# Reversing the column order in which TensorE streams the activations, and in which it writes PSUM

## The reference, cut to what matters

```python
def swiglu_ffn(h, w_gate_up, w_down):
    gate, up = jnp.split(h @ w_gate_up, 2, axis=-1)
    return (jax.nn.silu(gate) * up) @ w_down
...
u = h @ w_in                              # s5_mixer
val, gate = jnp.split(z @ w_glu, 2, axis=-1)
ckv = h @ w_kv_a; c_q = rms_norm(h @ w_q_a, q_a_norm)
q = c_q @ w_q_b; kv = c_kv @ w_kv_b
x = x + o @ mla_w_o[j]                    # and w_in_2, w_out_2 in the second block
```

## Time and profile before

| | |
|---|---|
| median of 3 runs | 1853.35 us (1852.85 to 1853.47) |
| profiled execution: span from the first to the last instruction | 1850.4 us |
| what the runs' median has beside that span | 2.95 us |
| TensorE matmul busy | 1793.4 us (97%), 8806 records |
| TensorE weight loads busy | 1379.8 us (75%) |
| VectorE, ScalarE, GpSimd busy | 1078.9 us (58%), 838.5 us (45%), 209.3 us (11%) |
| mean granted TensorE clock | 0.990 of full speed |

### The profile page before, as it was taken

The page is one execution under the profiler, slowest core; times in us unless marked ns, Lnnn a source line. Parts: engine busy times, 40 slices in busy tenths (PEclk is TensorE's granted clock), DMA queues, the critical chain, the costliest instruction groups (busy, mean ns, idle before and its releaser), DMA issues.

```text
span 1850.4 us, 24262 instructions
## 1 busy us (share of the span) xinstructions
PE 1793.4 (97%) x8806; PEld 1379.8 (75%) x8806; DVE 1078.9 (58%) x1752; ACT 838.5 (45%) x1404; POOL 209.3 (11%) x293
## 2 busy tenths in 40 slices
PE   9889999999999999999999999999999999999997
PEld 6777878888887766677888888868766777866675
DVE  8883454444434767755444434466576676577666
ACT  5423344443223667644444322233467633256763
POOL 7980000000000000000000000023000202300010
PEclk9989999999999999999999999999999999999999
DMA  6322223232333111122222233323211122311111
GB/s 212 89 74 80 91 91 102 91 102 88 94 100 105 49 32 30 50 69 92 101 93 99 93 92 95 107 75 109 69 57 51 53 80 87 108 58 58 46 58 57
DMA packets 58765, 152.14 MB, mean 82 GB/s; under 512 B 17152, under 2 KB 22048, under 8 KB 58672
## 3 DMA queue, kind: packets, MB, share of 16 engines
q1 hardware_dynamic: 55120, 148.21, 24.7%
q0 software_dynamic: 3552, 2.70, 0.5%
HBM read 143.73 MB, written 4.19 MB: 80 GB/s over the span
## 4 chain that ended last, share of the span: by engine, by line
PE 85%; DVE 6%; ACT 4%; POOL 3%; issue 2%; DMA 0%; SPq 0%; DVEq 0%; ACTq 0%; POOLq 0%
PE bank L2060 18%; PE bank L2062 18%; PE bank L2061 18%; PE bank L2561 3%; PE bank L2563 3%; PE bank L2562 3%; PE bank L2514 2%; PE bank L2543 2%; PE bank L2544 2%; PE bank L2545 2%; PE bank L2287 1%; DVE wl L1268 1%; PE bank L2315 1%; PE bank L2576 1%; PE bank L2301 1%
## 5 line engine op out<-in xcount | busy, mean ns | idle before, releaser
L1268 DVE TENSOR_TENSOR wl<-raw,wh 128x1024 fp32r<-128x1024 f32 (+3 forms) x280 | 325.0, 1161 | 481.1 <-ACT wh L686 477.9
L686 ACT ACTIVATE wh<-raw 128x1024 fp32r<-128x1024 f32 (+3 forms) x280 | 279.3, 998 | 568.4 <-PE bank L2062 498.3
L2060 PE MATMUL bank<-xH,wh 128*128 128x512 f32 x872 | 342.3, 393 | 0.6 <-DVE wl L1268 0.6
L2061 PE MATMUL bank<-xL,wh 128*128 128x512 f32 x872 | 339.6, 389 | 0.0
L2062 PE MATMUL bank<-xH,wl 128*128 128x512 f32 x872 | 339.6, 389 | 0.0
L2060 PEld LDWEIGHTS bank<-xH,wh 128*128 128x128 f32 x872 | 163.9, 188 | 36.6 <-issue 2.9
L2061 PEld LDWEIGHTS bank<-xL,wh 128*128 128x128 f32 x872 | 163.9, 188 | 34.6 <-issue 1.0
L2062 PEld LDWEIGHTS bank<-xH,wl 128*128 128x128 f32 x872 | 163.8, 188 | 34.2
L2060 PE MATMUL bank<-hidH,wh 128*128 128x512 f32 x352 | 137.4, 390 | 0.0
L2062 PE MATMUL bank<-hidH,wl 128*128 128x512 f32 x352 | 137.0, 389 | 0.0
L2061 PE MATMUL bank<-hidL,wh 128*128 128x512 f32 x352 | 137.0, 389 | 0.0
(11 more groups left out here) (455 smaller groups left out, 3355.6 us busy)
## 6 DMA issues: line engine op xcount, KB each, us to landing
raw<-w_gu_dram SPq DMA_DIRECT2D x88, 512.0 KB, 3.2
raw<-w_p_dram SPq DMA_DIRECT2D x64, 512.0 KB, 3.3
raw<-w_dn_dram SPq DMA_DIRECT2D x32, 448.0 KB, 3.3
raw<-w_glu_dram SPq DMA_DIRECT2D x16, 512.0 KB, 3.4
raw<-w_dn_dram SPq DMA_DIRECT2D x16, 512.0 KB, 3.6
raw<-w_out_dram SPq DMA_DIRECT2D x16, 512.0 KB, 3.2
raw<-w_in_dram SPq DMA_DIRECT2D x8, 512.0 KB, 7.7
raw<-w_o_dram SPq DMA_DIRECT2D x8, 512.0 KB, 3.3
```

Of the source, the lines that this page charges most:

```text
L686: nc.scalar.activation(wh[:, (st.base + u) % 2, 0:kts * P], raw[:, (st.base + u) % 4, 0:kts * P], ACT.Copy).then_inc(w_high, 1)
L1268: nc.vector.tensor_tensor(wl[:, s, 0:kts * P], raw[:, (st.base + u) % 4, 0:kts * P], wh[:, s, 0:kts * P].bitcast(F32), ALU.subtract).then_ ...
L2060: nc.tensor.matmul(bank, wh[:, s, w], hi[:, k, :], start=first and kt == 0, stop=False)
L2061: nc.tensor.matmul(bank, wh[:, s, w], lo[:, k, :], start=False, stop=False)
```

## The change

In the straight branch of `product` the streamed tile is read from column 511 down to column 0, and the bank is written from column 511 down to column 0. Column t of the tile still lands in column t of the bank. The weights, the order of the matmuls, their number, the waits and the signals are as before. All other matmuls keep their direction.

```diff
@@ product, straight branch
-                    nc.tensor.matmul(bank, wh[:, s, w], hi[:, k, :], start=first and kt == 0, stop=False)
-                    nc.tensor.matmul(bank, wh[:, s, w], lo[:, k, :], start=False, stop=False)
-                    ins = nc.tensor.matmul(bank, wl[:, s, w], hi[:, k, :], start=False, stop=last and kt == kts - 1)
+                    nc.tensor.matmul(bank[:, ::-1], wh[:, s, w], hi[:, k, ::-1], start=first and kt == 0, stop=False)
+                    nc.tensor.matmul(bank[:, ::-1], wh[:, s, w], lo[:, k, ::-1], start=False, stop=False)
+                    ins = nc.tensor.matmul(bank[:, ::-1], wl[:, s, w], hi[:, k, ::-1], start=False, stop=last and kt == kts - 1)
```

## The result

| | before | changed |
|---|---|---|
| median | 1853.2 us (1852.85 to 1853.47) | 1876.8 us (1875.55 to 1879.86) |
| ratio | | 1.0130, 95% interval 1.0118 to 1.0141 |
| span of the profiled execution | 1850.4 us | 1874.2 us |

The change makes the kernel 1.3% slower. The profiled execution of the changed kernel took 1875.96 us in all, 1.8 us more than its span. The prediction had put 2.95 us there, the difference between a median and the span of one execution; the 1.2 us between the two figures decide nothing.

A forecast was written before the change was run, and what follows sets the result against it. TensorE's pace was taken to bound the kernel. The one term, 4704 matmuls times a distance change of 0, added nothing to the 1850.4 us span; 2.95 us between median and span gave 1853.4 us, range 1835 to 1920 us.

The forecast's parts named there:

- What bounds the kernel: Whole kernel: TensorE's own pace sets the time, 97% busy; 1066 us, 58% of the span, hangs on the edited lines.
- the single term: Edited lines 2060 to 2062: 4704 matmuls times d, the change in distance between starts; 1 ns is 4.70 us.
- I take d = 0: Edited matmuls: distance between starts stays 226.6 ns, nothing changes beyond 0.2%; 1853.4 us, chance 0.51 including a normalised-away reversal.
- the repeated column: Warm-up matmuls, line 2200, stream one column 512 times at 0.433 us a pass, taken as showing an odd step costs nothing.
- Rival B: Edited matmuls: mirrored stream meets the weight load at a dearer position; 26.5 us, 1880 us, up to 1916; chance 0.23.
- coarse position does not matter: Feed-forward: weight slices at 0, 512, 1024 and 1536 B all run at 226.6 ns beside xH; argued against a dearer position.
- Rival C: Edited matmuls get faster: 744 on out-of-line tiles give -4.5 us, 1849 us; at most -56 us, 1797 us; chance 0.09.
- Rival D: SBUF fetch or PSUM write doesn't pair falling columns: full effect 950 us, 2804 us; partial 1920 to 2804; chance 0.17.

The follow-up runs named there:

- blocks_of_64: Against the kernel before, read and write of the 4704 matmuls go through 64-column (256 B) blocks in falling order, columns rising inside: 1853.0 us, ratio 0.9998.
- the second probe: Separate kernel, no reference result: rows of 48 float32 matmuls varying column order, position and weight columns; 226.7 ns between starts rising, 233.3 falling.
- the probe: Separate kernel, no reference result: rows of 48 matmuls, reads or writes reordered, float32 or bfloat16; float32 226.7 ns rising, 233.5 read falling, 226.9 write falling.

## Why the prediction was wrong in its forecast and right in its range

**What bounds the kernel, and the single term.** Right. Nothing but TensorE's pace changed, no cover existed, and the sum "4704 matmuls x d" is the loss: the changed lines took 27.2 us more, 5.8 ns each on average.

**"I take d = 0."** This step failed. Its reasons were that a falling stream touches the same aligned pairs and groups of columns, makes the same number of fetches, and that the repeated column shows no price. The first is shown to be free by itself: swapped pairs and falling order within 16 B cost nothing. What I left out is the order of the 16-byte pieces within 256 B, which blocks_of_64 and the groups of the second probe show to be the whole price; in the feed-forward d measured +6.7 ns. The second, the number of fetches, no run shows. The third reason rested on rows at the two-cycle pace, which have 2 ns beyond their columns' time where the edited lines have 13, and on a stream that never leaves its 16-byte piece; I should have given it no weight. It stood at 0.51 and should have been below B.

**Rival B.** It happened, at the price that I worked out from w_o: 26.5 us, 1880 us, against 27.2 us on the changed lines and 1876.8 us. I had it at 0.23, held down by "coarse position does not matter". That was read from slices at 0, 512, 1024 and 1536 B, all multiples of 256 B, and the second probe shows that positions repeat after 256 B (226.7 ns with the weights at 0 B and at 256 B), so those rows could not speak on it. Its mechanism was half right: a rising stream does depend on its position against the weights. But the falling stream does not get to 233.3 ns by starting at byte 2044, as a rising one does by lying 96 B off. It is there at nearly every position of stream and weights. So the price of B came true in part by luck: the row that I took it from was the rising pace at 96 B, 233.3 ns, and the other positions off the line would have given 228.8 to 234.5. That falling streams have one pace wherever they lie is also why w_o and w_glu hardly moved, which the sum for B had right by leaving out their 744 matmuls. The range held because it had been drawn to take in B.

**Rival C.** That no direction goes below 226.6 ns held in all positions and orders of 512 distinct float32 columns tried. Its smaller half, 4.5 us for the tiles that are out of line, was real, but came by moving the tiles (3 us), and not by the change.

**Rival D and the write.** Excluded at its full size on both sides: no order of 512 columns in these runs came near the two-cycle pace of 429 ns, two columns swapped within their pair are read at 226.7 ns and written at 227.7, and a falling write has 226.9. What is left of it on the read is the 6.7 ns of this change, below D's range. "PSUM — Partial Sum Buffer" of the Trainium skill, Specifications, was weighed against the change. For a step of 2 the probe agrees with it: 256 bfloat16 columns take 215.0 ns in place of 109.2. A step of -1 is not a non-contiguous write in that sense: 226.9 ns against 226.7. "SBUF — State Buffer" of the Trainium skill, Door 1, asks for two hits on a 16-byte line. The float32 read with a step of 2 has two hits and takes 229.7 ns for 256 columns where contiguous ones take 120.2, so the rule doesn't hold for that form; and the falling stream, which hits each line four times, pays all the same.

**Left open.** Shown is that the pace depends on order and position within 256 B, that for a rising stream the position of the weights counts, and that a bfloat16 stream with bfloat16 weights doesn't pay in any of the four directions tried. Not shown is what meets with what. A wait at some shared part of SBUF between the stream and the weight load would fit the relative position, but not that one weight column costs the falling stream as much as 128. One rival stands untested: no run has the weights in falling order beside a falling stream, so it may be the order of the two against each other that costs, and not the stream's own.

## What to carry to other kernels

Where matmuls of 4-byte streams of some 350 columns or more set the time, place the streamed tiles and the weights at the same position within 256 B and stream in rising order: 96 B of difference cost this kernel 33 us, and putting four tiles in line gave 3 us. A reversed PSUM write, a reversal of blocks of 256 B, swapped neighbours and a full reversal in bfloat16 were free here, so a reversal that is needed can be put there. And when a trace shows two paces for one instruction, the cheaper one is a favourable case that an edit can lose: such a row belongs to the forecast and not only to the range.

## What the runs showed of the hardware that was not expected

One float32 column repeated 512 times streams at 218.9 ns (the expectation for the second probe has 217.8 by mistake), 512 different ones at 226.7. Falling order inside groups of 16 columns costs 266.6 ns, 40 ns more than rising order and 33 more than falling, and nothing here explains it. A start 4 B off, in the middle of a 16-byte piece, costs 236.4 ns in rising order. With 8 weight columns a rising stream has 226.6 ns, with 16 and with 1 it has 231.
